# A band product and its exponentials made two rounds ahead in a chunked RWKV-7 scan

## The reference, cut to what matters

```python
def step(S, inp):                      # per head, 64 x 64 state
    r_t, w_t, k_t, v_t, a_t, b_t = inp
    sa = jnp.einsum('bhij,bhj->bhi', S, a_t)
    S = (S * w_t[..., None, :] + v_t[..., :, None] * k_t[..., None, :]
         + sa[..., :, None] * b_t[..., None, :])
    return S, jnp.einsum('bhij,bhj->bhi', S, r_t)
# a = -kk, b = kk * a_d, k = k_d, decay w = exp(-exp(logw)), both directions;
# 128 context tokens, 256 latent tokens, 16 heads
# modulation: m = silu(cvec) @ ada_w[layer] + ada_b[layer]   (1024 x 6144 a layer)
```

## Time and profile before

| | us |
|---|---|
| Median of 3 runs | 1508.85 (1502.84 to 1514.56) |
| Profiled execution, its own time | 1497.86 |
| Profiled execution, span | 1496.1 |
| TensorE busy in the span | 1276.4 (85%) |
| Scan, from its first product (193) to its last (620) | 427 |

### The profile page before, as it was taken

One profiled execution on the slowest core, in us unless ns is written; L12 is line 12 of the kernel. 1 busy time (PEld: TensorE's weight loads), 2 busy tenths in 40 slices (PEclk: granted clock), 3 DMA queues, 4 the chain that ended last, 5 costly groups with the idle time before them and its releaser, 6 DMA issues. The chain is left out here.

```text
span 1496.1 us, 21672 instructions
## 1 busy us (share of the span) xinstructions
PE 1276.4 (85%) x8627; PEld 894.2 (60%) x8627; DVE 527.0 (35%) x1159; ACT 325.4 (22%) x801; POOL 387.4 (26%) x708
## 2 busy tenths in 40 slices
PE   4699979999999888799577798979997794888897
PEld 2355845877888777535344455655685452555656
DVE  2800066556655654363510011320025525011115
ACT  2100153332222220031311111111116403111111
POOL 0100065554455432100024223000006601233310
PEclk9899988999999988589789999979997996999997
DMA  9922034766566224206369977847220073877752
GB/s 327 305 94 103 1 122 152 218 212 193 161 212 210 55 62 138 102 1 232 124 256 401 366 261 272 291 100 162 85 85 0 2 285 121 312 261 264 262 186 85
DMA packets 200852, 264.80 MB, mean 177 GB/s; under 512 B 93771, under 2 KB 155611, under 8 KB 185136
## 3 DMA queue, kind: packets, MB, share of 16 engines
q1 hardware_dynamic: 163200, 221.63, 44.2%
q0 software_dynamic: 17152, 31.20, 5.7%
q10 hardware_dynamic: 20400, 10.59, 3.3%
HBM read 300.22 MB, written 28.96 MB: 220 GB/s over the span
## 5 line engine op out<-in xcount | busy, mean ns | idle before, releaser
L2016 PE MATMUL psum<-ring,slab 128*64 128x256 f32 x896 | 192.7, 397 | 34.1 <-DMA slab<-moe_w,slab 31.7
L2016 PE MATMUL psum<-slab 128*64 128x256 f32 x832 | 174.0, 385 | 0.0
L2016 PEld LDWEIGHTS psum<-ring,slab 128*64 128x64 f32 x896 | 117.0, 144 | 94.1 <-issue 54.9
L2016 PEld LDWEIGHTS psum<-slab 128*64 128x64 f32 x832 | 108.1, 139 | 3.6 <-issue 1.0
L2044 PE MATMUL psum<-ring,ws 128*64 128x512 f32 x224 | 94.1, 595 | 17.1 <-issue 15.2
L2189 DVE TENSOR_TENSOR ws<-ws,psum 128x256 f32<-128x256 f32 (+1 forms) x28 | 17.1, 612 | 229.6 <-PE psum L2016 229.6
L2260 PE MATMUL psum<-slab,ring 128*128 128x384 f32 x256 | 85.5, 498 | 7.2 <-PEq L172 7.2
L2453 POOL TENSOR_SCALAR ws<-ws 128x384 f32<-128x384 f32 x32 | 39.4, 1243 | 190.8 <-DVE ws L2523 190.8
L2044 PE MATMUL psum<-slab,ws 128*64 128x512 f32 x208 | 87.5, 598 | 1.3 <-issue 1.3
L2108 POOL DMA_INDIRECT y_rows<-slab x26 | 26.4, 1015 | 228.1 <-DVE slab L2199 228.1
L622 PE MATMUL psum<-slab,ring 128*128 128x384 f32 x256 | 82.7, 486 | 0.0
(11 more groups left out here) (360 smaller groups left out, 2356.5 us busy)
## 6 DMA issues: line engine op xcount, KB each, us to landing
ring<-moe_w SPq DMA_DIRECT2D x84, 1024.0 KB, 7.0
ring<-ada_w SPq DMA_DIRECT2D x46, 1024.0 KB, 9.6
ws<-inverses SPq DMA_DIRECT2D x48, 256.0 KB, 4.0
slab<-moe_w SPq DMA_DIRECT2D x12, 1024.0 KB, 8.5
ring<-na_w_qkv SPq DMA_DIRECT2D x12, 1024.0 KB, 8.1
slab<-y_rows SPq DMA_DIRECT2D x12, 512.0 KB, 6.3
ring<-rwkv_w_r SPq DMA_DIRECT2D x4, 1024.0 KB, 8.4
ring<-rwkv_w_k SPq DMA_DIRECT2D x4, 1024.0 KB, 6.7
```

Of the source, the lines that this page charges most:

```text
L2016: last = nc.tensor.matmul(k.psum[BT * g:BT * g + BT, h_bank(s, kind), 0:DE], cols_[s % 2][:, c, BT * g:BT * g + BT], w[g][:, c, :], start= ...
```

## The change

- `bands(r + 2)` is multiplied at the end of round r, after the outputs, into bank 2 of each direction. It no longer waits for masks. ScalarE copies it at once into the buffer of `rate`. `pairs` of half `g = 0` waits for that copy, and so does the modulation product behind it, for direction 0.
- The exponentials that it needs are taken within round r: the reader's behind the copy of `r`, the key's behind the copy of `u`. VectorE's two multiplications a direction stand ahead of and behind the copy of the half solution (L1331).
- The modulation product at the end of round r is of block r + 1 and not r + 2, so it stands in rounds 0 to 8; `modulate(1)` is out of the opening, its weights are loaded in round 0, and `select(r)` stands in round r.
- The opening is reordered: bands 1 in it, the centring in three parts with the last behind the multiplications for round 1, squares summed in smaller groups at other places (bank 1).
- `solve` has a scratch and a transposed solution of its own and waits for no reader of `tmp`; `rates(r + 2)` waits until bands r + 1 are stored.
- The constant for the mean is set by GpSimd and not loaded, and TensorE's wait for that load is gone. The mask for `lower` is kept in bf16 on 64 partitions, and the head-sum table is a window of 30 columns.

```diff
-            act.dma_start(k.mean[:], a["c_mean"]).then_inc(masks_in, 16)
...
+            nc.gpsimd.memset(k.mean[:], 1.0 / D).then_inc(sig_c, 1)
...
-            pe.wait_ge(masks_in, 16)
...
-    def following(step, q, d):
-
-        step, q = (step, q + 1) if q < 3 else (step + 1, 0)
-        return q, TILE[step][d]
+    def place(r, d):
+
+        return ROUNDS[r][1], TILE[ROUNDS[r][0]][d], r % 2
...
+    CENTRES = [(0, 2), (2, 4), (4, DC)]
...
-    sums = k.psum[:, 6, 0:48]
+    sums = k.psum[:, 1, T:T + 48]
...
-            self.tmp_square = lent[0:64, 1024:1280].rearrange("p (i j) -> p i j", i=16)
...
-            self.band = self.u
+            self.band = lent[:, 1280:1536].rearrange("p (u n) -> p u n", u=4)
...
-    small, scratch = D2[0].square, D2[0].tmp_square
-    solution, solution_t = D2[1].square, D2[1].tmp_square
+    small, solution, solution_t = D2[0].square, D2[1].square, k.solution_t[:].rearrange("p (i j) -> p i j", i=16)
...
                 odd = r % 2
                 for d in range(2):
                     pe.wait_ge(first_ok[d], 2 * r + 2)
-                    if r:
-                        pe.wait_ge(a_ok[d], 4 * r - 2)
...
-                            last = nc.tensor.matmul(k.psum[:, b.bank + 1, P * (2 * e + c):P * (2 * e + c) + P], sides[d], sides[1 - d],
+                            last = nc.tensor.matmul(k.psum[:, b.bank + 2, P * (2 * e + c):P * (2 * e + c) + P], sides[d], sides[1 - d],
...
             rates_in(0, 2)
-            sum_squares(0)
+            sum_squares(0, 2)
             rates_in(2, 6)
+            pe.wait_ge(kk_floored, 1)
+            sum_squares(2, 4)
             pe.wait_ge(kk_inverse, 1)
             casts(0, 2)
             bands(0)
-            rates_in(6, 10)
-            sum_squares(1)
+            pe.wait_ge(nkk_ok, 1)
+            sum_squares(4, 7)
+            rates_in(6, 8)
+            sum_squares(7, DC)
+            rates_in(8, 12)
+            pe.wait_ge(band_ok[0], 2)
             modulate(0)
-            rates_in(10, 12)
             pe.wait_ge(kk_inverse, 2)
-            for d in range(2):
-                pe.wait_ge(band_ok[d], 2)
             casts(2, 4)
             rates_in(12, 14)
...
             last.then_inc(state_turned, 1)
-            select(0)
-            pe.wait_ge(sel_ok, 1)
-            modulate(1)
+            pe.wait_ge(ada_ok, 1)
+            pe.wait_ge(band_ok[1], 2)
+            bands(1)
             pe.wait_ge(state_ok, 2)
             pe.wait_ge(nkk_ok, DC)
...
                 for d, b in enumerate(D2):
                     pe.wait_ge(rest_ok[d], 2 * r + 2)
                     pe.wait_ge(y_ok[d], 2 * r + 2)
-                    if r == 0:
-                        pe.wait_ge(band_ok[d], 2)
-                    elif r <= 4:
+                    if 1 <= r <= 4:
                         pe.wait_ge(s_copied[d], r)
                     pairs(b, odd, 1, a_done[d])
-                    if d == 0 and r + 1 < MOD_PAIRS:
-                        select(r + 1)
+                    if d == 0 and r < MOD_PAIRS:
+                        if r == 0:
+                            pe.wait_ge(band_ok[0], 4)
+                        select(r)
                 for d, b in enumerate(D2):
-                    if d == 0 and r + 1 < MOD_PAIRS:
-                        pe.wait_ge(sel_ok, r + 2)
+                    if d == 0 and r < MOD_PAIRS:
+                        pe.wait_ge(sel_ok, r + 1)
+                    pe.wait_ge(band_ok[d], 2 * min(r + 2, len(ROUNDS)))
                     pairs(b, odd, 0, a_done[d])
-                if (step, q) != LAST:
-                    bands(r + 1)
                 for i, l in enumerate(LEVELS):
                     for d, b in enumerate(D2):
                         if i == 0:
...
                     last.then_inc(y_done[d], 1)
-                if r + 2 < MOD_PAIRS:
-                    modulate(r + 2)
+                if r + 2 < len(ROUNDS):
+                    bands(r + 2)
+                if r + 1 < MOD_PAIRS:
+                    pe.wait_ge(band_ok[0], 2 * min(r + 3, len(ROUNDS)))
+                    modulate(r + 1)
 
...
             roots(1)
             sigmoids(10, 16)
+            rows_copy(0)
+            for d in range(2):
+                act.wait_ge(centred[d], 2)
+                exps(d, *place(1, d), (0, 2))
             for d, b in enumerate(D2):
-                act.wait_ge(centred[d], 2)
+                act.wait_ge(centred[d], 3)
                 nc.scalar.activation(k.ep0[:, d, :, :], b.p[:, :, :, 0], ACT.Exp, scale=DECAY).then_inc(edges_ok, 1)
                 nc.scalar.activation(k.epe[:, d, :, :], b.p[:, :, :, P], ACT.Exp, scale=-DECAY).then_inc(edges_ok, 1)
-            for d in range(2):
-                exps(d, *following(0, 0, d), 1, (0, 2))
...
-                if r and (step, q) != LAST:
-                    for d in range(2):
-                        act.wait_ge(y_done[d], r)
-                        exps(d, *following(step, q, d), 1 - odd, (0, 2))
-                if r + 1 < MOD_PAIRS:
-                    rows_copy(r + 1)
-                    mod_copy(r + 1)
                 if (step, q) != LAST:
                     for d in range(2):
-                        exps(d, *following(step, q, d), 1 - odd, (1,))
-                    band_copy(r + 1)
+                        if r:
+                            act.wait_ge(y_done[d], r)
+                        exps(d, *place(r + 1, d), (1,))
+                if r < MOD_PAIRS:
+                    if r:
+                        rows_copy(r)
+                    mod_copy(r)
...
                 for d, b in enumerate(D2):
                     act.wait_ge(r_done[d], r + 1)
                     nc.scalar.copy(b.r.rearrange("p (e c) n -> p e (c n)", e=2), k.psum[:, b.bank:b.bank + 2, 0:P]).then_inc(r_ok[d], 1)
+                    if r + 2 < len(ROUNDS):
+                        exps(d, *place(r + 2, d), (0,))
                 for d, b in enumerate(D2):
                     act.wait_ge(u_done[d], r + 1)
-                    if (step, q) != LAST:
-                        act.wait_ge(band_out[d], 32 * r + 64)
                     nc.scalar.copy(b.u.rearrange("p u n -> p (u n)"), k.psum[:, b.bank + 2, 0:256]).then_inc(u_ok[d], 1)
+                    if r + 2 < len(ROUNDS):
+                        exps(d, *place(r + 2, d), (2,))
                 if step == 0:
                     for d, b in enumerate(D2):
                         act.wait_ge(s_done[d], r + 1)
                         if q:
                             act.wait_ge(s_out[d], 32 * q)
                         nc.scalar.copy(b.s_ctx.rearrange("p c n -> p (c n)"), k.psum[:, b.bank + 1, 0:P]).then_inc(s_copied[d], 1)
+                if r + 2 < len(ROUNDS):
+                    band_copy(r + 2)
...
-                if r:
-                    dve.wait_ge((solved, z_out)[d], (SOLVE * r, 32 * r)[d])
...
-                lo, hi = (NT * c for c in BATCH[b])
+                lo, hi = (NT * c for c in CENTRES[b])
...
             for d in range(2):
-                scaled_first(d, 0, TILE[0][d], 0, 0)
+                scaled_ar(d, 0)
+                scaled_kb(d, 0)
             for d in range(2):
-                scaled_rest(d, 0, TILE[0][d], 0, 0)
-            scans(2, 6)
+                scaled_rest(d, *place(0, d), 0)
+            scans(2, 4)
+            centre(1)
             floor(1)
+            scans(4, 6)
+            invert(1)
             scans(6, DC)
-            invert(1)
-            centre(1)
             divide(1)
+            dve.wait_ge(nkk_ok, DC)
+            for d in range(2):
+                scaled_ar(d, 1)
+                scaled_kb(d, 1)
+            centre(2)
...
-            dve.wait_ge(nkk_ok, DC)
-            for d in range(2):
-                scaled_first(d, *following(0, 0, d), 1, 1)
             for step, q in ROUNDS:
                 odd = q % 2
                 r = 4 * step + q
                 more = (step, q) != LAST
-                if r and more:
-                    for d in range(2):
-                        scaled_first(d, *following(step, q, d), 1 - odd, r + 1)
...
-                        scaled_rest(i, *following(step, q, i), 1 - odd, r + 1)
+                        scaled_rest(i, *place(r + 1, i), r + 1)
+                ahead = r + 2 < len(ROUNDS)
+                if ahead:
+                    scaled_ar(0, r + 2)
+                    scaled_ar(1, r + 2)
+                    scaled_kb(0, r + 2)
                 for d, b in enumerate(D2):
                     dve.wait_ge(half_done[d], r + 1)
                     nc.vector.tensor_copy(b.r[b.late].rearrange("p u n -> p (u n)"), k.psum[b.late, b.bank + 1, 0:256]).then_inc(half_ok[d], 1)
+                if ahead:
+                    scaled_kb(1, r + 2)
                 for d, b in enumerate(D2):
...
-                pool.wait_ge(rest_ok[0], 2 * r + 2)
...
-                pool.wait_ge(rest_ok[1], 2 * r + 2)
...
-                rates(d, 0, TILE[0][d])
+                rates(d, 0)
             squares(5, DC)
```

(11 more changed lines are left out.)

104 lines of the change are left out of this document (53 added, 51 removed).

## The result

The changed kernel takes **1532.1 us** (median of 4 runs, 1512.9 to 1551.2) beside 1505.8 for the kernel before on the same chip: a ratio of **1.0155 [1.0082, 1.0229]**. Measured once more on another chip it was 1.0224 [1.0154, 1.0294]. It is slower, by 1.5 to 2.2%, and both intervals are clear of 1; predicted were 1508.9 us and a range up to 1527. Ratios leave out single executions over 1.5% above the fastest of their kernel, medians keep them, and as the ones left out have a lower clock (0.888 for 1551.2 us beside 0.917 for 1512.9), the two can differ by over half a percent.

A forecast was written before the change was run, and what follows sets the result against it. Middle rounds were bound by TensorE's path through modulation and pairs, then VectorE's masks, at full clock. Terms -1.6 - 3.0 + 3.0 + 19.5 - 1.7 - 0.5 - 15.6 = +0.1 gave a median of 1508.9 us, range 1494 to 1527.

The forecast's parts named there:

- the middle round ends: Ends of rounds 0 to 7: bands and the wait for their copy delay modulation, pairs and masks; +19.5 us.
- It held through round 10, which began with longer waits than that: Argument that the last round keeps full clock, because round 10 kept it; supports 26.12 us for that round.
- Opening: Before the scan's rounds: modulation out, part of the centring in, -3.0 us; first pairs at half clock, +3.0 us.
- Start: Program start: the transposes no longer wait for the mean to be loaded; -1.6 us.
- Last round: Round 11: the wait for the inverse is hidden and the clock holds; 26.12 us where it was 41.68, -15.6 us.
- End 8: End of round 8: gains a modulation, loses a DMA wait and half clock; 32.35 us where it was 34.06, -1.7.
- End 9: End of round 9: bands, masks and the rest of the path take 26.98 us where it was 27.49, -0.5.
- ScalarE's and VectorE's moved work at nothing: Within rounds: four exponentials and three multiplications moved there fit into gaps and waits; cost 0.
- SyncE and GpSimd at nothing: Reordered stores and loads, and rates and solve waiting for a band's store, add no time to the rounds; cost 0.
- slow round 0: Rival: round 0 stays at half clock after the opening; +17 us over the sum, 1526 us, chance 0.20.
- The last round's wait: Rival: the inverse comes no sooner, so round 11 keeps its wait and half clock; +15.6 us, 1524 us, chance 0.10.
- the bands were not free: Rival judged: bands at round ends fall into TensorE's waiting and the modulation's wait is hidden; -20 us, 1489 us, chance 0.12.

The follow-up runs named there:

- The kernel with the second gap filled: Changed kernel plus seven unread transposes before the first level's second products, where TensorE waits 0.95 us for VectorE; ratio 1.0030 to the kernel before.
- candidate 3: Changed kernel with bands of rounds 1 to 9 at their old place, copied into the solution's buffer, and late-round gaps filled with transposes; 0.9854 to the kernel before.
- the kernel with all bands at the old place: Changed kernel with bands of rounds 1 to 11 again one round ahead, behind the next round's pairs, in the first level's bank; ratio 1.0033 to the kernel before.
- the kernel with the other bank: Changed kernel with bands of rounds 2 to 5, 10 and 11 in bank 1, so modulation there skips the copy wait; ratio 1.0148 to the kernel before.

## Why the prediction was wrong

**The step that failed** is the one for the middle round ends, 8 x 2.52 - 0.7 = +19.5, in what it left out: it took the clock of these rounds as 1.00, as in the earlier trace rows. I had TensorE's new wait in my own list ("TensorE idle for about a microsecond before L989") and gave it no price, since it lay on the path already. It cost nothing as a wait and 5.9 or 1.2 us as the place of a fall: 13.0 us in the profiled execution, 28.5 over rounds 1 to 8 in the second (3 x 5.86, 4 x 1.24, one of 5.9), where rounds 10 and 11 lost 11.8 each besides (38.31 for 26.5, 37.63 for 25.8). The kernel with the second gap filled shows that the falls come with this wait, and that without them the kernel is where I had put it.

**The mechanism behind the 19.5** was right and the size a little high: 2.42 for 2.69 up to `modulate`, 2.22 for 2.52 a round, 16.9 for 19.5 in all (29.9 less 13.0). Of it the wait for the copy is 0.87, as reckoned above; I had 0.77 + 0.33.

**"It held through round 10, which began with longer waits than that"** was no evidence. One execution in which the clock held says little: the same round of the same kernel took 27.5 us in one profile and 41.0 in another, with transposes elsewhere.

**Opening:** 4.5 instead of 3.0 for the stretch to `pairs`, and round 0 at half clock +2.65 for +3.0, with the clock back by the first level. **Start:** -2.2 for -1.6. **Last round:** -14.5 for -15.6; it had a short fall, and without one it takes 25.8 us, 0.3 under my 26.12. That the term is so large is luck of the profile that I started from: 13.2 of it is the half clock of one execution, and another execution with the same last round took 33.68, not 41.68. **End 8:** 33.35 with a short fall, 32.1 without; predicted 32.35. **End 9:** 27.85 and 26.5 for 26.98. **ScalarE's and VectorE's moved work at nothing:** right, by candidate 3. **SyncE and GpSimd at nothing:** no wait of TensorE for a DMA is left in rounds 1 to 8, and the rounds without a fall leave no room for more than the bands and their copy; they were not tested apart.

The rivals: slow round 0 placed the clock's risk in one round, at the opening; what the runs show is the same risk in every round, behind its new wait. The last round's wait was gone, the bands were not free. My sign for the last round, clock 1.00 and 26 us, did not come: 0.94 and 27.17. After the scan the changed kernel lost another 4.1 us in code that is the same; that part took from 872 to 893 us over the profiles here, so this is not put down to the change.

**What stays open:** why a fall at the same place costs 5.9 us in one round and 1.2 in another, in the same execution too, what picks the rounds that fall, and what of the opening's better 1.5 us comes from which edit. Filling the opening up to the first `pairs` without rest was not tried.

## What to carry to other kernels

Where one engine was busy without a break, price a new wait twice: as time, and as a gap after which its clock may fall; in this kernel the second price was the larger (13 and 28 us in rounds 1 to 8, beside some 7 for the wait for the copy and nothing for the other). Look through all executions' times, not at one profile, before saying that the clock holds. Find out which gap the falls follow before filling any: here one of two mattered, and filling that one cost nothing. When a part is put back for an experiment, look for what its waits now move (here GpSimd's product, 0.58 us a round) before the rest is put down to the change.

## What the hardware showed unexpectedly

- TensorE went to 1.2 GHz behind a wait of 0.95 us in rounds in which it is 93% busy without a fall (30.56 of 32.70 us), and in other executions of the same instructions it did not. A wait alone does not decide it: in round 4 of the kernel with all bands at the old place TensorE waited 1.07 us for the inverse, ahead of the same narrow products, and the clock stayed at 1.00.
- A fall at the same instruction took some 13 us at half clock (round at 37.4 for 31.5) or some 4 us (34.0 for 32.75) in the changed kernel, in one execution the same over several rounds in a row, in the other not. In the kernel with the other bank one lasted to nearly the end of its round (43.78 for 32.02).
- Seven 128x128 transposes (0.93 us) in that gap held the clock in rounds 1 to 8 of all three profiles that had them there. Fourteen in round 9 of the kernel before, which has longer waits, did not: they took 3.09 us, where fourteen take 1.75 at full clock.
- VectorE's product of two SBUF operands, 128x256, took 0.66 and 0.83 us beside a GpSimd product of the same shape, 0.42 alone.
